# Four weight tiles at each visit of the modulations, and two banks kept from x's last attentions until the values' products have them

## What is computed

```python
for i in range(DEPTH):                              # DEPTH = 2
    mod   = s_lat @ w_mod[i] + b_mod[i]             # 6 x 1024 numbers, from c alone
    mod_c = s_ctx @ w_mod[i] + b_mod[i]
    h  = rms_norm_2(x,  norm_mix[i]) * (1.0 + sc1)  + sh1
    hc = rms_norm_2(xc, norm_mix[i]) * (1.0 + sc1c) + sh1c
    y, yc = token_mixers(h, hc, w_in[i], w_out[i], ...)   # recurrence, neighbourhood and window attention
    x = x + g1 * y
    x = x + g2 * swiglu(rms_norm_2(x, norm_ffn[i]) * (1.0 + sc2) + sh2, ...)
    if i < DEPTH - 1:                               # the same for the context, in layer 0 only
        xc = xc + g1c * yc
        xc = xc + g2c * swiglu(...)
```

## Time and profile before

| | us |
|---|---|
| median of the three runs | 1896.7 |
| the profiled execution's own time | 1903.14 |
| its span (first to last instruction) | 1901.8 |
| TensorE busy in it | 1812.8 |
| VectorE busy | 1267.8 |
| ScalarE busy | 995.9 |
| granted TensorE clock, mean share of full speed | 0.983 |

### The profile page before, as it was taken

The page is one execution under the profiler, slowest core; times in us unless marked ns, Lnnn a source line. Parts: engine busy times, 40 slices in busy tenths (PEclk is TensorE's granted clock), DMA queues, the critical chain, the costliest instruction groups (busy, mean ns, idle before and its releaser), DMA issues. The chain is left out here.

```text
span 1901.8 us, 35689 instructions
## 1 busy us (share of the span) xinstructions
PE 1812.8 (95%) x14792; PEld 1673.5 (88%) x14792; DVE 1267.8 (67%) x2327; ACT 995.9 (52%) x1744; POOL 79.2 (4%) x78
## 2 busy tenths in 40 slices
PE   7999899999999999999989999999999989889997
PEld 6877799978888899899989887999999988589997
DVE  4555655568787755766776767676765668766665
ACT  4563544456555654644755645454664455444443
POOL 0000200010000200000200100000100000100000
PEclk8998999999999999999999999999999989899999
DMA  9677766887433455455555443455655533245653
GB/s 329 238 266 238 272 184 217 264 294 231 131 118 108 154 185 189 134 166 172 157 174 167 131 159 106 133 172 179 198 165 168 178 111 104 64 120 180 186 180 122
DMA packets 93825, 334.92 MB, mean 176 GB/s; under 512 B 10960, under 2 KB 12880, under 8 KB 93536
## 3 DMA queue, kind: packets, MB, share of 16 engines
q1 hardware_dynamic: 92016, 327.33, 54.0%
q0 software_dynamic: 1648, 5.31, 0.9%
HBM read 331.55 MB, written 1.05 MB: 175 GB/s over the span
## 5 line engine op out<-in xcount | busy, mean ns | idle before, releaser
L555 DVE TENSOR_TENSOR low<-ring,high 128x1024 fp32r<-128x1024 f32 x410 | 502.3, 1227 | 230.0 <-ACT high L547 216.9
L580 PE MATMUL bank<-XHx,high 128*128 128x256 f32 x2096 | 612.0, 292 | 21.2 <-DVE low L555 10.9
L581 PE MATMUL bank<-XLx,high 128*128 128x256 f32 x2096 | 595.4, 284 | 0.0
L582 PE MATMUL bank<-XHx,low 128*128 128x256 f32 x2096 | 595.2, 284 | 0.0
L547 ACT CAST high<-ring 128x1024 fp32r<-128x1024 f32 x410 | 427.9, 1044 | 292.1 <-PE bank L582 254.1
L580 PEld LDWEIGHTS bank<-XHx,high 128*128 128x128 f32 x2096 | 402.9, 192 | 42.8 <-issue 21.5
L581 PEld LDWEIGHTS bank<-XLx,high 128*128 128x128 f32 x2096 | 404.0, 193 | 1.3 <-issue 0.2
L582 PEld LDWEIGHTS bank<-XHx,low 128*128 128x128 f32 x2096 | 403.9, 193 | 0.0
L580 PE MATMUL bank<-XHc,high_side 128*128 128x256 f32 x608 | 177.7, 292 | 7.8 <-DVE low_side L555 7.7
L581 PE MATMUL bank<-XLc,high_side 128*128 128x256 f32 x608 | 170.9, 281 | 0.0
L582 PE MATMUL bank<-XHc,low_side 128*128 128x256 f32 x608 | 170.6, 281 | 0.0
(11 more groups left out here) (448 smaller groups left out, 3071.8 us busy)
## 6 DMA issues: line engine op xcount, KB each, us to landing
ring<-in_stream SPq DMA_DIRECT2D x410, 512.0 KB, 3.7
ring_side<-in_stream SPq DMA_DIRECT2D x110, 512.0 KB, 3.7
ring_mod<-in_stream SPq DMA_DIRECT2D x96, 512.0 KB, 5.8
x_nb<-in_rpb POOLq DMA_DIRECT2D x6, 256.0 KB, 3.8
x_late_NB<-in_rpb POOLq DMA_DIRECT2D x6, 256.0 KB, 3.2
Xx<-in_x SPq DMA_DIRECT2D x2, 512.0 KB, 6.0
Xc<-in_ctx SPq DMA_DIRECT2D x1, 1024.0 KB, 7.6
out<-y SPq DMA_DIRECT2D x8, 128.0 KB, 2.0
```

Source lines behind the costliest of these rows:

```text
L555: nc.vector.tensor_tensor(st.low[:, j % st.n_ring, :], st.ring[:, j % st.n_ring, :], st.high[:, j % st.n_split, :].bitcast(F32), ALU.subtr ...
L580: nc.tensor.matmul(out, wh, xh, start=(i == 0), stop=False)
L581: nc.tensor.matmul(out, wh, xl, start=False, stop=False)
L582: m = nc.tensor.matmul(out, wl, xh, start=False, stop=(c == ks[-1]))
```

## The change

```diff
 class Slots:
-    def __init__(self, k, ids, state=None):
-        self.k, self.ids = k, list(ids)
+    def __init__(self, k, ids, state=None, later=(), once=None):
+        self.k, self.first, self.later, self.once = k, list(ids), list(later), once
         self.state = {} if state is None else state
...
         while True:
-            at = min(self.ids, key=order)
+            more = self.once is None or self.once in marks
+            ids = self.first + self.later if more else self.first
+            at = min(ids, key=order)
             after, _ = self.state.get(at, (None, 0))
             if after is None or after in marks:
                 break
-            yield [self.state[i][0] for i in self.ids]
+            yield [self.state[i][0] for i in ids] + ([] if more else [self.once])
...
         x.gemm, x.banks, x.wide = (Slots(self, ids, state) for ids in ((0, 1), (5, 6, 7), (5, 6, 7, 0, 1)))
-        x.all = Slots(self, range(8), state)
+        x.attention = [Slots(self, ids, state, (0, 1), (("att V", "x", layer), "product", NQ - 1))
+                       for layer, ids in enumerate(((5, 6, 7), range(2, 8)))]
         c.gemm = c.banks = c.wide = Slots(self, (2, 3, 4), state)
...
-MOD_US, MOD_BATCH = 0.43, 2
+MOD_US, MOD_BATCH = 0.43, 4
...
-    banks, ahead = {("x", 0): (w.wide, 1), ("x", 1): (k.px.all, 2), ("c", 0): (w.wide, 0)}[path, layer]
+    banks, ahead = {("x", 0): (k.px.attention[0], 1), ("x", 1): (k.px.attention[1], 2), ("c", 0): (w.wide, 0)}[path, layer]
```

## The result

The changed kernel takes 1906.0 us (median of 12 runs, 1900.0 to 1909.9) where the kernel before takes 1897.4 in the same session (12 runs, 1892.1 to 1902.2). The ratio is 1.0048, 95% interval 1.0037 to 1.0060: **slower by some 8.6 us**. A second set of the same two kernels gave 1.0047 (1.0030 to 1.0063). The prediction had said 5.2 us faster, 1891.5 us, and a range of 1883 to 1903; the time lies 3 us above its upper end, and the direction is that of the rival "slower" (0.20).

A forecast was written before the change was run, and what follows sets the result against it. TensorE's work plus 89 us of its idle time was taken as the bound. Gains of 0.9 (visits), 3.4 (layer 1) and 0.9 (layer 0) summed to 5.2 us off, from 1896.7 to 1891.5 us, range 1883 to 1903.

The forecast's parts named there:

- the rival "slower": At 126 to 206 us, whole-ring visits starve the fillers: twelve tiles move, waits double; 1905.4 us, or 1902; chance 0.20.
- The price of a visit: Modulation visits on TensorE cost 1.19 us for two tiles, 2.05 for four; joining two saves 0.33 us.
- How many are joined where it counts: In dense stretches outside the three filler stretches, 24 visits become 12, gaining 4.0 us; upper bound 7.9.
- What it takes away: In the three filler stretches, 6 tiles fewer fit and move to dense stretches at 0.51 us each: 3.1 us back.
- My cycle of 9.5 us per four tiles: In the filler stretches, one whole-ring round of visit, landing and queued loads was taken as 9.5 us.
- TensorE's waits for modulation tiles: 6.6 us in 9 times, in the filler stretches, counted as nothing; up to another 6.6 us lost as bound.
- The clock: At 126 to 170 us, clock 0.84 (0.54 in 145 to 150) would go on falling; argued for the slower rival, unpriced.
- Layer 1, the bank: `ATT_V` waits for a score bank; with banks 2 to 7 for scores it starts 3.5 us sooner, gaining 3.4; lower bound 0 or 1 lost.
- the signs against me: Under 28 filler tiles, over 10 us tile waits, clock well under 0.84, or `ATT_V` at once but attention's end unmoved.
- the first two are 3.6 us and can go: In layer 1 before the values' first use, idle stretches of 1.14 and 2.49 us can vanish; the third, 1.34, stays.
- Layer 0: The same wait, 1.79 us idle before `ATT_V`'s preceding turns; half taken as gain, 0.9 us, between 1.8 faster and 2 slower.
- The plan found anew: The rest of the plan may shift either way; 3 us allowed, with no sign.

The follow-up runs named there:

- banks_l0: Kernel before plus the bank rule in x's layer 0 alone, layer 1 as before, two tiles a visit: 1894.7 us, 0.9989 of the kernel before.
- hyst_l0: `banks_l0`, but once behind their pace the modulations stay first in rank until four tiles are done: 1904.3 us, 1.0033 of the kernel before.
- cap48: `banks_l0`, but no modulation tile beyond the 48th as a filler in planned time 100 to 262 us: 1913.0 us, 1.0084 of the kernel before.
- nofill_b4: Bank rule in layer 0 alone, four tiles a visit, modulations never as fillers, only when due: 1933.8 us, 1.0193 of the kernel before.
- nofill_b2: `banks_l0` with modulations never as fillers, only when due, two tiles a visit: 1928.7 us, 1.0168 of the kernel before.
- mp500: `banks_l0` with the modulations' pace stretched from 480 to 500 planned us: 1899.5 us, 1.0007 of the kernel before.
- quiet4: Changed kernel plus 50 unread 128 x 128 matmuls in planned TensorE gaps of the first two stalls: 1900.9 us, 1.0024 of the kernel before.
- banks: Kernel before plus the bank rule of both layers, modulations still two tiles a visit: 1897.1 us, 1.0002 of the kernel before.
- after_again: The changed kernel itself measured once more, as the control for `quiet4`: 1906.1 us, 1.0047 of the kernel before.
- quiet2: `banks_l0` plus 15 unread 128 x 128 matmuls in planned TensorE gaps of the first two stalls: 1896.9 us, 0.9996 of the kernel before.
- b4_l0: `banks_l0` with four tiles a visit instead of two: 1903.8 us, 1.0035 of the kernel before.

## Why the prediction was wrong, point by point

Four steps failed. The credit for joined visits (12 joined, 4.0 us) was too large, since the saving shows in one stretch only, as 1.5 us. The tiles that leave the stalls were 10 and not 6. TensorE's clock was put at nothing where it made some 3 to 5 us. And the 3.4 us for layer 1 were idle time that moved instead of going.

**The price of a visit: right.** 1.19 us for two tiles and 2.05 for four were read from rows, and six kernels bear them out in the dense stretch m40 to m100, against `banks_l0`'s 183.0 us with nine visits of two (10.7 us):

```
           visits      by the prices   measured
hyst_l0     5 x four       -0.5          -0.5
after       7 x four       +3.6          +5.7
cap48      16 x two        +8.3          +7.7
nofill_b4   9 x four       +7.7          +7.6
nofill_b2  20 x two       +13.1         +12.5
mp500       7 x two        -2.4          -2.4
```

What after has over its price, 2.1, is mostly work that came sooner: 20 products with `hidden` operands (250 or 251 of each kind for 244) less 7 of the main stream's, 13 x 0.12 = 1.6 us. The next stretch, with 20 fewer of them, gives part of it back (-0.6). `quiet4`, with 12 fewer of these products in the dense stretch than after, took 187.2 there: 12 x 0.12 = 1.4 less.

**How many are joined where it counts: wrong.** I credited 12 joined visits, 4.0 us. All tiles outside the three filler stretches stood for "dense" in my count. But ten of those visits lie before 120 us, and there nothing was gained. Window of 0 to 126 in before, then after:

```profile
0.00:126.00 126.00, 112.61 (x852) 95.01 (x853) 63.43 (x144) 66.75 (x124) 1.47 (x6) 0.96 0.79 277
```

```profile
0.00:126.00 126.00, 111.72 (x862) 96.23 (x863) 63.47 (x146) 68.04 (x128) 1.47 (x6) 0.99 0.79 276
```

The mark m28 is a fair place to compare, since 24 modulation tiles are used before it in both kernels. It stands at 124.2 in before and 124.3 in `banks`, at 124.6 in after and 124.1 in `after_again`. By prices the joined visits should have brought it 1.65 us forward. It isn't that TensorE has idle time there: of the 13 idle us in before nearly all lie in the first 30, and from 30 to 126 before's trace shows TensorE busy throughout. What the trace does show is that after does 12 more small instructions before that mark (ten `SQc,c_meanD`, two transposes), which before does later, in the stalls. At 0.12 us each they would be 1.4 us; that they used up the saving is an estimate, and no run isolates it. So the saving can be read only for the nine visits between m40 and m100; joined they are 4.5 pairs, 4.5 x 0.33 = 1.5 us. I had tested one window, 206 to 300, and taken it for all.

**What it takes away: the mechanism right, the size wrong.** By m40 60 tiles are used in before and 52 in after, and between m100 and m120 18 and 16. The dense stretch between them has to take 28 instead of 18: 10 displaced, where I had 6. In price 10 x 0.51 = 5.1 instead of 3.1 us. With the 1.5 this makes +3.6 us in the dense stretch, which is the row of after in the table. My cycle of 9.5 us per four tiles was right where the ring was the limit: in after the visits of the first stall start at 126.70, 132.19 (its four tiles in four pieces, each waiting for its load), 145.75 and 154.82, so two cycles take 19.05 us and the third 9.1. What is missing is a fifth visit. The next one starts at 185.6, while `banks` still puts four tiles into the gap at 157.00 (rows above). Why the planner found no place for four there, no run isolates.

**TensorE's waits for modulation tiles: right to count nothing.** Waits of after and of `banks` (us, times):

```profile
  PEld bank L719: 6.5, 6
  PE bank L719: 3.7, 6
```

```profile
  PEld bank L719: 11.0, 12
  PE bank L719: 5.4, 11
```

They fell. The "slower" rival, which doubled them, had the right sign and the right place, 126 to 206 us, but the wrong second term: what came on top of the tiles was not the wait. That its 1905.4 us lie 0.6 from the measured time is luck.

**The clock: left out, and roughly half of the loss, within wide bounds.** I had the row (0.54 in 145 to 150) and put it on the rival's side without a price. `quiet4` prices it: of 8.8 us over before (control) 5.2 go when the gaps are filled, with the wide interval given above. The mean granted clock over all runs points the same way: 0.9825 for after (18 runs), 0.9852 for `quiet4`, 0.9857 for before beside them. 0.0027 of 1900 us is 5.1 us if every matmul that ran at half speed was on the path. Among the 29 runs of before in that session a straight line gives 1.3 us for each 0.001 of clock, so 0.0027 would be some 3.5 us; this is an estimate. What is left in `quiet4`, 1.0024 or 4.5 us, are by its marks +2.4 in the stalls, +4.2 in the dense stretch and +1.4 in the third stall, less what comes back behind m120. How the 2.4 divide between longer visits in the chain's way and clock that is still missing (0.96 for 0.98) stays open.

**Layer 1, the bank: wrong.** As forecast, `ATT_V` begins at once. As I had also listed among the signs against me, the attention's end did not come sooner. TensorE's timeline in after, to be held against the earlier trace rows:

```profile
1608.92 0.28 PE L587 MATMUL bank<-XHx,low 128*128 128x256 f32 x1
1609.04 1.03 PE L878 MATMUL bank<-c_ident,x_late_T 128*128 128x128 f32 x8
1609.91 0.60 PE L1046 MATMUL bank<-x_sq,c_rot 128*128 128x256 f32 x2
1610.16 0.58 PE L624 MATMUL bank<-high,XHx 128*128 128x512 f32 x1
...
1619.28 1.06 PE L878 MATMUL bank<-c_ident,x_late_T 128*128 128x128 f32 x8 [2.06 <-DVE x_late_T L975]
...
1624.81 0.62 PE L624 MATMUL bank<-high,XHx 128*128 128x512 f32 x1 [2.54 <-DVE low L560]
...
1636.19 1.08 PE L903 MATMUL bank<-x_late_PT,c_v 128*64 128x256 f32 x8 [1.34 <-ACT x_v L1075]
```

From the last product to `ATT_V`'s first are 1.24 us instead of 3.56, 2.3 sooner and not 3.5. The rule does this: the distance is 1.24 in the four profiles with it in layer 1 (`banks`, after, `after_again`, `quiet4`) and 3.55 or 3.56 in the ten without. So a bank was the cause of the late start, though not by the read that I named. VectorE's read at 1611.44 ends at 1612.19, after `ATT_V` has begun; the one before it ends in time:

```profile
1610.77 0.74 DVE L930 CUSTOM_DVE_ANT_0 x_late_T<-bank,c_window,smallx 128x512 f32<-128x512 f32 x1
```

But from that product to the values' first are 27.3 us instead of 26.3. Over all profiles it is 26.7 to 28.4 with the rule and 24.6 to 26.3 without, of which the clock makes some (1.00 where it was 24.6, 0.93 or 0.94 at 26.2 and 26.3, 0.88 at 28.4). The 1.14 us of idle are gone, but 2.06 stand ahead of a later set of turns instead, for VectorE's scaling (L975). The 2.49 us of idle that I had let go are there again, 2.54, for the same reason: `ATT_V`'s next tiles are not split. VectorE's timeline shows where they wait:

```profile
1622.22 0.68 DVE L935 CUSTOM_DVE_ANT_0 x_late_T<-bank,x_late_NB 128x512 f32<-128x512 f32 x1
...
1623.44 3.49 DVE L560 TENSOR_TENSOR low<-ring,high 128x1024 fp32r<-128x1024 f32 x3
```

Three splits in a row, behind the scores of the next pair. An `ATT_V` that starts sooner runs into the same late splits, and waits. The step that failed was "the first two are 3.6 us and can go": both hung on VectorE, and I had named the releaser of each from its row. Together they are 4.6 us now. The marks m290 to m409 give the rule 0 to 1 us lost, inside my lower bound.

**Layer 0: not shown.** I forecast 0.9 us. m200 to m290 took 576.5 in before, and 575.9, 574.7 and 572.6 in `banks`, `banks_l0` and `quiet2`, which have one order there and still differ by 3.3 us. In after itself it took 578.0, in `after_again` 578.7 and in `b4_l0` 577.5, 1 to 2 us longer than in before. The stretch holds side products too, so none of this prices the rule alone.

**The plan found anew.** I allowed 3 us with no sign. Three small shifts (`mp500`, `hyst_l0`, `cap48`) each took 5 to 7 us more than `banks_l0` between m120 and m290, 2 to 4 more than before. The three profiles of four-tile visits in after's order took 969.2 there (median) for 971.7 in the other group, so this had no part in the miss; but 3 us were too narrow an allowance.

**In sum**, by m120 and in medians: +4.4 in the stalls (how much of it is clock stays open), +5.6 in the dense stretch, -0.6 in the third stall; behind it a gain of 1 us or so. Forecast were -0.9, and -4.3 for the attentions. One step of the chances doesn't follow either: 1892.9 us lies seven tenths up the forecast's own band of 1888 to 1895, not nine.

## What to carry to other kernels

Here work that fills stalls was worth more in small pieces. A bigger visit showed its 0.33 us in one dense stretch only; a saving has to be read for each stretch in which it is claimed, not for one. Idle time ahead of TensorE cost twice, once as itself and once as the low clock of the work behind it (4.17 us, then 2.4 more on 24 matmuls); price both. Where nothing useful fits into a gap a dummy matmul can pay (5.2 us in `quiet4`), and where few gaps are left it doesn't (`quiet2`). When a wait is removed, look at the releaser of the next one: if it hangs on another engine's queue, the time only moves.

## What the hardware showed that I had not expected

One program with one order of instructions ends its second stall at 211.8 us in one execution and at 216.7 in another, the granted clock 0.91 and 0.83 between 120 and 210 us; the dense stretch behind it took 188.7 and 188.5. So a single pair of profiles says little about a stretch with gaps (the profile of before stands 6.0 us behind `banks` at m40 with the same order), and very much about a dense one: 183.0 five times out of five (`quiet2` too).
